# Issuing the 64-column products of a two-block model kernel by halves of their output rows

## The reference

```python
# block 1: RWKV-7 mixer (8 heads of 64, chunks of 128 tokens), retention mixer, gated merge, conv FFN
# per chunk n and head:   rhs = A_kv @ v (+ zr @ state)      128 x 64
#                         sa  = inv(I - L) @ rhs             128 x 64
#                         y   = B_v @ v + B_a @ sa (+ r @ state)
# block 2: Mamba-2 mixer (32 heads of 64, 4 groups, chunks of 128)
#   y_diag[i] = sum_j (c_i . b_j) * decay[i, j] * x_dt[j]     128 x 64 for each head and chunk
# block 2: sliding-window attention (16 query heads of 64, 4 key heads, window 128, with sinks)
#   out = softmax(q k^T) v, the sum of the exponentials kept as a 65th column of v
# and between them: per-layer embeddings, norms, FFN and all dense projections
```

## Time and profile before

| what | value |
|---|---|
| median of 3 runs | 935.45 us (935.07 to 939.02) |
| profiled execution | 936.12 us, of which the span is 934.3 us |
| TensorE matmul busy | 899.6 us, 96% of the span |
| VectorE busy | 678.2 us, 73% |
| ScalarE busy | 510.9 us, 55% |
| matmuls | 5801, with as many weight loads |
| DMA | 136.63 MB, 146 GB/s on average |

### The profile page before, as it was taken

The page is one execution under the profiler, slowest core; times in us unless marked ns, Lnnn a source line. Parts: engine busy times, 40 slices in busy tenths (PEclk is TensorE's granted clock), DMA queues, the critical chain, the costliest instruction groups (busy, mean ns, idle before and its releaser), DMA issues.

```text
span 934.3 us, 14617 instructions
## 1 busy us (share of the span) xinstructions
PE 899.6 (96%) x5801; PEld 786.6 (84%) x5801; DVE 678.2 (73%) x968; ACT 510.9 (55%) x732; POOL 81.4 (9%) x83
## 2 busy tenths in 40 slices
PE   6999999999999989999999899999999998999998
PEld 5998988988888769999988699988888786878777
DVE  6688737856868678898854668787686777776665
ACT  7863332243535376665643565765565666577553
POOL 6002402300000000000000000007320000000000
PEclk9999999999999989999999999999999999999999
DMA  9543222122555455565555454552323544532231
GB/s 310 171 149 105 92 91 90 47 92 90 195 188 179 149 168 181 189 208 189 183 190 197 153 172 147 185 180 90 112 82 123 176 151 153 204 105 91 91 116 64
DMA packets 80979, 136.63 MB, mean 146 GB/s; under 512 B 3957, under 2 KB 46545, under 8 KB 80912
## 3 DMA queue, kind: packets, MB, share of 16 engines
q1 hardware_dynamic: 78800, 131.17, 42.1%
q0 software_dynamic: 2112, 4.53, 1.6%
HBM read 134.64 MB, written 1.05 MB: 145 GB/s over the span
## 4 chain that ended last, share of the span: by engine, by line
PE 63%; DVE 6%; ACT 6%; issue 3%; DMA 1%; DVEq 0%; ACTq 0%
PE bank L443 18%; PE bank L445 17%; PE bank L444 17%; PE bank L432 3%; DVE lower L1903 2%; ACT upper L1333 2%; PE bank L1112 1%; PE bank L917 1%; PE bank L925 1%; PE bank L1096 1%; DVE arena L2456 1%; ACT arena L1819 1%; DMA loaded<-in_ffn_w_up 1%; DMA loaded<-in_ple_gate_w 1%; ACT arena L1432 1%
## 5 line engine op out<-in xcount | busy, mean ns | idle before, releaser
L1903 DVE TENSOR_TENSOR lower<-loaded,upper 128x2048 fp32r<-128x2048 f32 x122 | 278.6, 2287 | 123.8 <-ACT upper L1333 121.7
L1333 ACT ACTIVATE upper<-loaded 128x2048 fp32r<-128x2048 f32 x122 | 231.9, 1903 | 115.3 <-PE bank L445 99.0
L443 PE MATMUL bank<-xT_upper,upper 128*128 128x256 f32 (+1 forms) x664 | 186.5, 281 | 2.7 <-DVE lower L1895 1.6
L444 PE MATMUL bank<-xT_lower,upper 128*128 128x256 f32 (+1 forms) x664 | 185.0, 279 | 0.0
L445 PE MATMUL bank<-xT_upper,lower 128*128 128x256 f32 (+1 forms) x664 | 184.9, 278 | 0.0
L443 PE MATMUL bank<-upper,xT_upper 128*128 128x512 f32 (+1 forms) x360 | 146.7, 407 | 4.6 <-DVE lower L1903 3.4
L445 PE MATMUL bank<-upper,xT_lower 128*128 128x512 f32 (+1 forms) x360 | 139.9, 389 | 0.0
L444 PE MATMUL bank<-lower,xT_upper 128*128 128x512 f32 (+1 forms) x360 | 139.3, 387 | 0.0
L443 PEld LDWEIGHTS bank<-xT_upper,upper 128*128 128x128 f32 (+1 forms) x664 | 125.1, 188 | 4.1 <-DVE lower L1895 1.8
L444 PEld LDWEIGHTS bank<-xT_lower,upper 128*128 128x128 f32 (+1 forms) x664 | 125.3, 189 | 0.2
L445 PEld LDWEIGHTS bank<-xT_upper,lower 128*128 128x128 f32 (+1 forms) x664 | 125.2, 189 | 0.1
(11 more groups left out here) (349 smaller groups left out, 1167.9 us busy)
## 6 DMA issues: line engine op xcount, KB each, us to landing
loaded<-in_w_in SPq DMA_DIRECT2D x26, 1024.0 KB, 5.1
loaded<-in_ffn_w_up SPq DMA_DIRECT2D x22, 1024.0 KB, 5.1
loaded<-in_ssm_in_w SPq DMA_DIRECT2D x20, 1024.0 KB, 5.2
loaded<-in_ffn_w_down SPq DMA_DIRECT2D x11, 1024.0 KB, 4.9
loaded<-in_ssm_out_w SPq DMA_DIRECT2D x8, 1024.0 KB, 4.9
loaded<-in_ple_gate_w SPq DMA_DIRECT2D x8, 1024.0 KB, 5.0
loaded<-in_attn_in_w SPq DMA_DIRECT2D x8, 1024.0 KB, 5.2
loaded<-in_w_branch_ret SPq DMA_DIRECT2D x4, 1024.0 KB, 4.9
```

The costliest lines, as they stand in the source:

```text
L443: mm(out, a[0], b[0], start=start, stop=False)
L444: mm(out, a[0], b[1], start=False, stop=False)
L1333: A(part(upper, PARTS, n), part(loaded, LOADS, n), ACT.Copy).then_inc(uppers, 1)
L1903: TT(part(lower, LOADS, n), part(loaded, LOADS, n), part(upper, PARTS, n).bitcast(F32), sub) \
```

## The change

A helper `halves` issues a product as two: the first with weight columns 0 to 63, which writes the output rows 0 to 63, the second with weight columns 64 to 127, which writes rows 64 to 127. Both stream the same operand and have all 128 contraction rows. It is used for all products of `rhs`, `sa` and `y`, the state products among them (these stream 128 columns), for the diagonal and for the values. Order of heads, banks, waits and increments are as before; the last half carries the increment.

```diff
+            def halves(out, a, b, start, stop):
+                for c in (slice(0, 64), slice(64, P)):
+                    last = mm(out[c], a[:, c], b, start=start, stop=stop)
+                return last
...
-                for p in range(4):
-                    if n:
-                        mm(ps[:, P * p:P * p + P], zr[:, p, n, 0:P], s0[:, p, :], start=True, stop=False)
-                    for o in range(2):
-                        hd = 2 * p + o
-                        last = mm(ps[:, 64 * hd:64 * hd + 64], mats[:, hd, 2, :], vrow[:, n, 64 * hd:64 * hd + 64],
-                                  start=(n == 0), stop=(n == 0 or o == 1))
+                for hd in range(8):
+                    c = slice(64 * hd, 64 * hd + 64)
+                    if n and hd % 2 == 0:
+                        halves(ps[:, 64 * hd:64 * hd + P], zr[:, hd // 2, n, 0:P], s0[:, hd // 2, :], True, False)
+                    last = halves(ps[:, c], mats[:, hd, 2, :], vrow[:, n, c], n == 0, n == 0 or hd % 2 == 1)
...
-                    last = mm(ps[:, 64 * hd:64 * hd + 64], invT[:, hd, :], rhs[:, 64 * hd:64 * hd + 64],
-                              start=True, stop=True)
+                    c = slice(64 * hd, 64 * hd + 64)
+                    last = halves(ps[:, c], invT[:, hd, :], rhs[:, c], True, True)
...
+                    halves(ps[:, c], mats[:, hd, 3, :], vrow[:, n, c], n == 0, False)
+                    last = halves(ps[:, c], mats[:, hd, 1, :], sa[:, c], False, n == 0 or hd % 2 == 1)
...
-                    last = mm(ps[:, 64 * e:64 * e + 64], wT[:, n, e, :], xd[:, n, 64 * hd:64 * hd + 64],
-                              start=True, stop=True)
+                    last = halves(ps[:, 64 * e:64 * e + 64], wT[:, n, e, :], xd[:, n, 64 * hd:64 * hd + 64], True, True)
...
-                        last = mm(ps[:, 65 * e:65 * e + 65], aeT[:, z % 2, P * (kt_ * e + s):P * (kt_ * e + s) + P],
+                        last = halves(ps[:, 65 * e:65 * e + 65], aeT[:, z % 2, P * (kt_ * e + s):P * (kt_ * e + s) + P],
                                   vv[:, s, 2 * u + o, :], start=(s == 0), stop=(s == kt_ - 1))
```

More of the change, by code:

```diff
@@ L751, in _ @@
                 ps = take(pe, ("y", n), 4)
[L752 to L759, removed]
+                for hd in range(8):
+                    c = slice(64 * hd, 64 * hd + 64)
+                    if n and hd % 2 == 0:
+                        halves(ps[:, 64 * hd:64 * hd + P], zr[:, hd // 2, n, P:2 * P], s0[:, hd // 2, :], True, False)
+                    halves(ps[:, c], mats[:, hd, 3, :], vrow[:, n, c], n == 0, False)
+                    last = halves(ps[:, c], mats[:, hd, 1, :], sa[:, c], False, n == 0 or hd % 2 == 1)
                 fill(last, ("y", n))
```

## The result

The changed kernel takes 928.78 us (median of 12 executions) against 936.53 for the kernel before (12), ratio 0.9915 with a 95% interval of 0.9897 to 0.9932. A second set gave 928.15 us and a ratio of 0.9906 (0.9873 to 0.9938). So the change wins 0.85 to 0.94%, some 8 to 9 us, where 15 were forecast: the direction and the range hold, the size is little more than half.

What follows compares the result with a forecast made beforehand. TensorE was taken as the bound nearly everywhere. Recurrence 6.8, diagonal 4.3 and values 4.7, less 0.8 for group starts, summed to 15.0 us saved: 920.5 us from the median 935.45, range 915.0 to 930.8.

Steps and rivals of the forecast that it cites:

- TensorE is the bound, and what it saves where it never waits is saved.: Whole kernel: matmuls cover 96% of the span, so a microsecond off TensorE where it never waits shortens the kernel equally.
- A pair with 128 weight columns costs 0.111, one with 64 costs 0.058, and two halves run side by side.: Recurrence, diagonal and values, 352 pairs: weight load sets the step, both halves together take 0.058 us, saving 0.053 a pair.
- The state products: Recurrence, 16 pairs streaming 128 columns: stream sets the step as much as the load, so halving brings 0.
- Rivals 3 and 4: Changed products: 3, halves take turns, 939.0 or 945.8 us, chance 0.12; 4, loads wait for other half's stream, 978, chance 0.02.
- The same PSUM bank: Changed products: doubt that halves run side by side, since both write one bank, unlike the overlapping products in the earlier trace.
- Going in and out of the narrower shape: 0.: Around every group of halves: no time lost, as around the 32-column product with all 128 rows.
- The other end of the bound: Around the groups: 0.34 us lost for each of 14, half that for the 12 values, 6.8 us in all.
- Rival 1: Around all groups of halves: going in and out costs 6.8 us, giving 927.3 us; chance 0.15.
- Three diagonals' saving goes into VectorE's waits, 4.3 us stay.: Diagonal's stage: of 6.8 us saved, the 2.5 from three diagonals before waiting transposes only lengthens those waits.
- Rival 2: Diagonals and values: other engines take most, about 3.5 us kept there together, recurrence's 6.8 stay, giving 926 us; chance 0.07.
- The clock: 1.7 us either way, nothing to the middle.: After the recurrence: half-clock stretches may get longer or shorter, one event costing at most 1.7 us, added to both ends.
- Values: 4.7.: Attention's values: 5.1 us saved on 96 pairs, less 0.4 beneath ScalarE's busy stretch, so 4.7 us stay.

Runs made afterwards that it cites:

- val_only: Halves in attention's values alone, all other products whole as in the kernel before; 936.09 us, ratio 0.9977 against the kernel before.
- two_whole_later: Changed kernel with the two diagonals ahead of the waiting transposes whole again, and `sa` of chunk 1 issued three times to shift it; 930.38 us, one execution.

## Why the prediction was right and wrong, point by point

- *TensorE is the bound, and what it saves where it never waits is saved.* Right: in the recurrence and the values the trace gives back what the groups give, 4.7 and 3.0 us, and all but 0.4 us of it is kept up to the end.
- *A pair with 128 weight columns costs 0.111, one with 64 costs 0.058, and two halves run side by side.* Right: 0.112, 0.058 and 0.029 per matmul of the two. The state products, which stream 128 columns, step by 0.056 as halves and 0.112 as a pair of halves, so their 0 was right too. Rivals 3 and 4 (in turn; loads behind streams) fall with that row. The same PSUM bank, named as a doubt, makes no difference (0.35 lost and 0.029 either way). The rule of the Trainium skill, "TensorE: Matmul & The Clock Gate", "The mechanism", that a load overlaps matmuls only of other row groups, disagrees with that step of 0.029 on common rows; the measurement decides.
- *Going in and out of the narrower shape: 0.* This is the first and larger step that failed. It was read off the only narrow product on 128 rows, which is float32r; the changed ones are float32. The other end of the bound, 0.34 from the earlier trace rows, was right: 6 groups of the recurrence x 0.34 = 2.0 us (forecast 6.8, measured 4.7), and in the values 12 x 0.15 = 1.8 (forecast 4.7, measured 3.0). In the diagonal's stage it brings a group that counts from 0.85 down to 0.51. Rival 1, given 0.15, described this and gave 927.3; the time is 928.8 and 928.2. The rule of the Trainium skill, "TensorEngine Tiling (Array Packing)", "Key Properties", that a change of tiling mode drains the engine, agrees with every float32 row here and not with the float32r ones.
- *Three diagonals' saving goes into VectorE's waits, 4.3 us stay.* The wait in front of step 10 grew as forecast (1.36 to 3.37, forecast about 3), and the one near 725 too. But more than three diagonals went into waits, and this is the second step that failed: five were to count, 0.85 each. The first saved nothing, because the carried product behind it waited 0.6 us for VectorE. The next two brought 1.04, of which the wait at step 10 took 0.7, since VectorE was late there by an operation of its own. Only the two behind it count in full, 0.51 each. So 1.3 us stay and not 4.3. Rival 2, given 0.07, described this part.
- *The clock: 1.7 us either way, nothing to the middle.* The three falls of before were thought of, a new one wasn't, though the forecast had the wait that brings it. It is 6.8 us at half the clock and costs 2.7 us, twice what the halves save in this stage, and more than the 1.7 that the range had for one event. One of the old falls, before 790, is absent in the changed kernel's trace and brings 1.5, and the one at 341 comes at a better moment and brings 0.9. Together they come to 0.3 us worse than the nothing in the sum. That is luck: one term of 2.7 that was not thought of, and two that another execution may not have.
- *Values: 4.7.* The 0.4 for ScalarE's busy stretch was about right (those waits grew by 0.4); the rest of the gap is the change of shape.
- The sum again, with the measured terms: recurrence 4.7, the stretch from 231 to 648 1.1 (0.9 of it the clock's), diagonal's stage 1.3 - 2.7 = -1.4, the absent fall 1.5, values 3.0, start and end of the trace -0.6, together some 8.4 us. Of the 6.6 us that are missing against 15.0, the change of shape takes the most.

## What to carry to other kernels

A product whose stream is shorter than its weight load can be issued as two column halves that run side by side, for 0.058 us a pair instead of 0.112, but going into the narrower shape and out again costs 0.34 us in float32: a group should hold well over 6 pairs (0.34 / 0.053), and what stands in it should all have the same shape. Take the price of a change from a row of the same type as the changed operation. And when a saving is expected to vanish in a wait, ask how long the wait gets, for behind a longer one the clock may fall and take more than was saved. Here moving other matmuls into the wait brought 3.0 us by the traces, and the halves of that stage 1.3.

## What the runs showed of the hardware that had not been expected

- A narrow float32r product costs nothing going in and out (0.01 us with 256 streamed columns, 0.06 with 64), a float32 one of the same size 0.34.
- Which of the array's columns a narrow product uses, and into which PSUM bank, makes no difference to that.
- A wait of 3.4 to 3.6 us was followed by a granted clock of 0.50 in all four kernels that had one there, for 3.4 us in three and 6.8 in one; of the kernels with 1.4 us it was two with a fall and three without; 1.78 and 1.09 us with matmuls between had none.
- Executions of the same instructions differ at a granted clock of 1.00: in val_only and two_whole_later some 110 us of dense matmuls ran about 4% slower than in the other traces (257 matmuls in 30 us against 268 in the kernel before).
